# A transformer of three blocks on one core: three weight slots and ten row places while expert rows come, five weight slots elsewhere, and another order in the first up block

## What is computed

```python
def peer_ffn(h, w_q, sub_keys, u_tab, v_tab):
        q = (xc @ w_q).reshape(t, PEER_HEADS, 2, PEER_QDIM // 2)
        sc = jnp.einsum('thpc,hpnc->thpn', q, sub_keys).astype(jnp.float32)
        v_half, i_half = lax.top_k(sc, PEER_TOPK_HALF)
        ...
        top_s, pos = lax.top_k(cand, PEER_TOPK)
        g = jax.nn.softmax(top_s, axis=-1)
        u = u_tab[expert]
        act = jax.nn.gelu(jnp.einsum('thkd,td->thk', u, xc).astype(jnp.float32), approximate=False)
        w = (g * act).astype(xc.dtype)
        return jnp.einsum('thk,thkd->td', w, v_tab[expert])
```

## Time and profile before

| | us |
|---|---|
| median of 3 runs | 2128.93 |
| lowest, highest | 2127.93, 2129.14 |
| profiled execution, device time | 2127.96 |
| span of the profiled execution | 2126.2 |
| PE busy, share of the span | 1665.4 (78%) |
| DVE busy | 1490.8 (70%) |
| ACT busy | 785.7 (37%) |
| POOL busy | 643.3 (30%) |
| DMA moved | 746.87 MB, mean 351 GB/s |
| mean granted clock of PE | 0.902 |

### The profile page before, as it was taken

The page is one execution under the profiler, slowest core; times in us unless marked ns, Lnnn a source line. Parts: engine busy times, 40 slices in busy tenths (PEclk is TensorE's granted clock), DMA queues, the critical chain, the costliest instruction groups (busy, mean ns, idle before and its releaser), DMA issues.

```text
span 2126.2 us, 20672 instructions
## 1 busy us (share of the span) xinstructions
PE 1665.4 (78%) x6490; PEld 1005.3 (47%) x6490; DVE 1490.8 (70%) x3129; ACT 785.7 (37%) x2050; POOL 643.3 (30%) x524
## 2 busy tenths in 40 slices
PE   8797777667777865887778478765767899999998
PEld 4473343622323453333344433554333465668986
DVE  5378876897756688976666897668787465566654
ACT  1213452234424422432452235212555343454432
POOL 0013444335433343643344354425444000000000
PEclk9999989879898987989889799987888999999999
DMA  7358999999999999999999999999999785574452
GB/s 274 148 213 365 421 399 421 419 421 422 418 421 401 416 421 411 413 420 421 416 373 421 412 389 421 421 421 422 400 412 392 308 306 202 194 281 160 178 178 99
DMA packets 105803, 746.87 MB, mean 351 GB/s; under 512 B 12896, under 2 KB 13536, under 8 KB 16608
## 3 DMA queue, kind: packets, MB, share of 16 engines
q0 software_dynamic: 73728, 536.90, 61.4%
q1 hardware_dynamic: 31536, 207.08, 25.1%
q10 hardware_dynamic: 432, 1.57, 0.2%
HBM read 744.46 MB, written 1.05 MB: 351 GB/s over the span
## 4 chain that ended last, share of the span: by engine, by line
PE 39%; DMA 23%; DVE 20%; ACT 10%; issue 6%; DVEq 1%; PEldq 1%; PEld 0%; ACTq 0%; SPq 0%; POOL 0%; POOLq 0%
DMA sb_work<-in_peer_uv,sb_expert 17%; PE ps_acc L1570 11%; PE bank L496 5%; DVE sb_work L1534 5%; PE bank L1363 4%; DVE sb_x L1542 3%; DMA sb_ninth<-in_peer_uv,sb_expert 3%; PE bank L2060 2%; DMA sb_wring<-in_peer_w_q 2%; ACT L1550 2%; PE bank L777 2%; PE bank L566 2%; PE ps_acc L566 2%; PE ps_acc L568 2%; PE ps_acc L567 2%
## 5 line engine op out<-in xcount | busy, mean ns | idle before, releaser
L2694 POOL DMA_INDIRECT sb_work<-in_peer_uv,sb_expert x456 | 567.8, 1245 | 916.8 <-PE ps_acc L1570 401.8
L1570 PE MATMUL ps_acc<-sb_work,sb_diag 128*128 128x512 f32 x1184 | 626.9, 676 | 255.3 <-ACT sb_diag L1559 218.2
L1534 DVE CUSTOM_DVE_ANT_0 sb_work<-sb_work,sb_h 128x1024 f32<-128x1024 f32 x456 | 551.0, 1222 | 147.9 <-DMA sb_work<-in_peer_uv,sb_expert 138.7
L1570 PEld LDWEIGHTS ps_acc<-sb_work,sb_diag 128*128 128x128 f32 x1184 | 242.9, 216 | 586.2 <-issue 577.1
L1550 ACT ACTIVATE sb_dots<-sb_dots 128x1 f32<-128x1 f32 x512 | 102.1, 199 | 501.8 <-DVE sb_dots L1534 471.2
L1542 DVE SCALAR_TENSOR_TENSOR sb_x<-sb_work,sb_weight,sb_x 128x1024 f32<-128x1024 f32 x160 | 205.0, 1281 | 72.3 <-ACT sb_weight L1551 72.3
L560 DVE TENSOR_TENSOR sb_work_r<-sb_wring,sb_work_r 128x2048 fp32r<-128x2048 f32 (+1 forms) x74 | 133.8, 1828 | 101.0 <-ACT sb_work_r L553 100.4
L1551 ACT ACTIVATE sb_weight<-sb_dots,sb_share 128x1 f32<-128x1 f32 x512 | 150.8, 294 | 16.6
L553 ACT CAST sb_work_r<-sb_wring 128x2048 fp32r<-128x2048 f32 (+1 forms) x74 | 111.8, 1536 | 108.8 <-PE ps_acc L568 39.1
L1363 PE MATMUL bank<-sb_hT,sb_wring 128*128 128x128 f32 x1024 | 125.0, 287 | 24.3 <-DMA sb_wring<-in_peer_w_q 21.8
L1363 PEld LDWEIGHTS bank<-sb_hT,sb_wring 128*128 128x128 f32 x1024 | 123.2, 203 | 27.7 <-issue 26.6
(11 more groups left out here) (362 smaller groups left out, 2391.1 us busy)
## 6 DMA issues: line engine op xcount, KB each, us to landing
sb_wring<-in_w_mix SPq DMA_DIRECT2D x36, 1024.0 KB
sb_wring<-in_peer_w_q SPq DMA_DIRECT2D x32, 1024.0 KB
sb_wring<-in_w_gate SPq DMA_DIRECT2D x32, 1024.0 KB
sb_wring<-in_w_up SPq DMA_DIRECT2D x16, 1024.0 KB
sb_wring<-in_w_down SPq DMA_DIRECT2D x16, 1024.0 KB
sb_wring<-in_mla_w_uq SPq DMA_DIRECT2D x12, 768.0 KB
sb_work<-in_hyb_w_in SPq DMA_DIRECT2D x8, 1024.0 KB, 14.7
sb_wring<-in_hyb_w_out SPq DMA_DIRECT2D x8, 1024.0 KB
```

What stands on the lines that cost most here:

```text
L1534: e.tensor_tensor_reduce(u, u, h[:, t, :], 1.0, 0.0, ALU.mult, ALU.add, dots[:, i:i + 1]).then_inc(dot_ready, 1)
L1570: last = e.matmul(ps_acc[:, b * 512:(b + 1) * 512], diag[:, number % DIAGS, :], row(n)[:, D + b * 512:D + (b + 1) * 512], start=k == f["fi ...
L2694: pool.indirect_dma_start(row(n), None, a["peer_uv"], bass.IndirectOffsetOnAxis(ap=expert[:, t, n % P:n % P + 1], axis=0)).then_inc(row_la ...
```

## The change

SLOTS becomes 3. `ninth` becomes `extra` with two pieces of a slot's size, and RING is 10. The two pieces belong to the weight stream before block 20 and from block 104 on, where it has five slots, and to the rows in between, as row places 8 and 9. A new function `place_stream` says for each block into which slot it goes and what it waits for; it takes the slot that was filled longest ago. Rows 8 and 9 wait until the last blocks in the two pieces (18 and 19) are given back, and the first blocks from 104 on in these pieces wait for the last rows there.

```diff
-SLOTS = 4
+SLOTS = 3
+EXTRA = 2
 KEPT = 8
-RING = 9
+RING = KEPT + EXTRA
...
+        def place_stream():
+            last = [None] * (SLOTS + EXTRA)
+            uses = [0] * (SLOTS + EXTRA)
+            for n in range(len(stream)):
+                open_slots = SLOTS if rows_from <= n < rows_until else SLOTS + EXTRA
+                if n == rows_from:
+                    for i in range(EXTRA):
+                        rows_after[KEPT + i] = last[SLOTS + i]
+                if n == rows_until:
+                    for i in range(EXTRA):
+                        last[SLOTS + i] = rows_until - 0.5
+                slot = min(range(open_slots), key=lambda s: -1 if last[s] is None else last[s])
+                if last[slot] == rows_until - 0.5:
+                    n_rows = len(gathers) * P
+                    behind = freed(max(r for r in range(n_rows) if r % RING == KEPT + slot - SLOTS))
+                else:
+                    behind = None if last[slot] is None else given_back[last[slot]]
+                placed[n] = slot, uses[slot], behind
+                last[slot] = n
+                uses[slot] += 1
...
-                if n >= SLOTS:
-                    sp.wait_ge(*given_back[n - SLOTS])
+                if placed[n][2] is not None:
+                    sp.wait_ge(*placed[n][2])
...
                 elif n < KEPT:
                     pool.wait_ge(*given_back["kept", n])
+                else:
+                    pool.wait_ge(*given_back[rows_after[n]])
```

Three smaller edits come with it. In the norm ahead of the first route, PE gets four 128x512 matmuls whose result nobody reads:

```diff
+            def pe(e):
+                for _ in range(4):
+                    e.matmul(ps_scores[:, 0:2, :].rearrange("p a b -> p (a b)"), ident[:, :], busy, start=True, stop=True)
+                p("pe", e)
```

In `project_last` block 7 is split instead of plain:

```diff
-            plain = (9, 0, 3, 7)
+            plain = (9, 0, 3)
```

In the first up block ACT takes the root ahead of its cast and both casts early, and DVE makes the scales ahead of its split:

```diff
             for b, (_, units, sq_v, _) in enumerate(up_plan):
-                split_act(e, next_splits[b][0])
                 if b == 0:
                     e.wait_ge(var_ready.sem, rows_var)
                     e.activation(root, var, ACT.Sqrt).then_inc(root_ready.sem, 1)
-                if b + 1 == len(up_plan):
+                split_act(e, next_splits[b][0])
+                early = b == 0 or b + 1 == len(up_plan)
+                if early:
                     split_act(e, next_splits[b][1])
...
             for b, (_, units, _, hi_v) in enumerate(up_plan):
+                if b == 0:
+                    scale_then(e)
                 split_dve(e, next_splits[b][0])
                 if b == 0:
-                    scale_then(e)
+                    spread_copy(e)
```

More of the change, by code:

```diff
@@ L193, in build @@
         diag = sb("diag", [P, DIAGS, P])
-        ninth = sb("ninth", [P, 2 * D])
-        w_landed = [sem(f"w_landed{i}") for i in range(SLOTS)]
+        extra = sb("extra", [P, EXTRA, SLOT])
+        w_landed = [sem(f"w_landed{i}") for i in range(SLOTS + EXTRA)]
         w_used = Signal(sem("w_used"))
@@ L244, in build @@
         stream = []
+        placed = {}
         given_back = {}
@@ L331, in slot_wait @@
                 return
-            pe.wait_ge(w_landed[n % SLOTS], 16 * (n // SLOTS + 1))
+            slot, use, _ = placed[n]
+            pe.wait_ge(w_landed[slot], 16 * (use + 1))
         def slot_flat(n):
             _, chunks, cols = stream[n]
-            return wring[:, n % SLOTS, 0:chunks * cols]
+            slot = placed[n][0]
+            home = wring[:, slot, :] if slot < SLOTS else extra[:, slot - SLOTS, :]
+            return home[:, 0:chunks * cols]
+        def place_stream():
[18 more added lines that the diff above has]
+                uses[slot] += 1
         def load_table(e, function):
@@ L358, in next_gain, with norm @@
                 load_gain(e, number + 1)
-        def norm(src, dst, width, g, tiles=range(TILES)):
+        def norm(src, dst, width, g, tiles=range(TILES), busy=None):
             act, dve, p, _ = norm_parts(src, dst, width, g, tiles)
-            stage(act=act, dve=dve, points=[p], us=5.0)
+            def pe(e):
+                for _ in range(4):
+                    e.matmul(ps_scores[:, 0:2, :].rearrange("p a b -> p (a b)"), ident[:, :], busy, start=True, stop=True)
+                p("pe", e)
+            stage(pe=None if busy is None else pe, act=act, dve=dve, points=[p], us=5.0)
         def norm_parts(src, dst, width, g, tiles):
@@ L1580, in row @@
         def row(n):
-            return ring[:, n % RING, :] if n % RING < KEPT else ninth[:, :]
+            return ring[:, n % RING, :] if n % RING < KEPT else extra[:, n % RING - KEPT, :]
         def freed(n):
@@ L1642, in feed_forward @@
         def feed_forward(layer, tiles, beside=None, halved=False):
-            norm(X, H, D, (f"ffn{layer}", a["ffn_norm"][layer:layer + 1, :]), tiles)
+            norm(X, H, D, (f"ffn{layer}", a["ffn_norm"][layer:layer + 1, :]), tiles,
+                 hT[:, 0:4, 0:P] if (layer, tiles) == (0, [0]) else None)
             turn_wide(H, hT, DC, tiles)
@@ L2579, in up_act @@
                     e.copy(hidden[0][b][:, j, :], units_2[:, (4 * b + j) % 8, :]).then_inc(turned_hi.sem, 1)
-                if b + 1 < len(up_plan):
+                if not early:
                     split_act(e, next_splits[b][1])
@@ L2603, in scale_then, with spread_copy @@
             last.then_inc(first_row.sem, 1)
+        def spread_copy(e):
             token_unit.wait_full(e)
@@ L2635, in build @@
         share_out()
+        place_stream()
         block = ctx.enter_context(nc.Block())
```

11 lines of the change are left out of this document (6 added, 5 removed).

## The result

The changed kernel takes 2166.65 us (median of 4 runs, 2164.69 to 2173.63) against 2129.03 us (4 runs, 2127.93 to 2130.85). The ratio is 1.0181, with a 95% interval from 1.0164 to 1.0198. That is 37.6 us slower. The prediction said 2156, between 2112 and 2184, and slower at 0.67. The profiled execution took 2165.37 us, with a span of 2163.5.

A forecast was written before the change was run, and what follows sets the result against it. DMA engines near 420 GB/s, with DVE almost full, bound the rows stage; PE the prologue and epilogue. Terms -3, -7.5, +28, +5, +10, -5 gave +27.5 on 2127.96, 2155.5, stated as 2156; range 2112 to 2184.

The forecast's parts named there:

- step E: project_first, nine pairs: three slots lengthen cycles until the row queue empties, then the lag limits itself; +10, 0 to +30.
- A: Prologue's norm: four busy matmuls keep PE's clock up for the first route's first matmuls; -3, between -4 and 0.
- B: Rows stage: tenth place fills gaps in two late windows (-5) and from 290 to 332 (-2.5); -7.5, between -10 and 0.
- The sign named for it: Rows stage: over 410 GB/s in the windows answering to 1500 to 1560 and 1600 to 1640 us.
- C: Three routes beside rows: later pairs wait, ACT's copy and DVE lag 11 each, 3, 2 and 0 hidden; +28, 0 to +40.
- D: Layer 1's two latent projections: w_uq blocks asked for one block's work later; +5 for both, between 0 and +13.
- F: Epilogue: split block 7 (-1.3), scales ahead of the split (-2.3), fifth slot for w_branch (-1.3); -5, between -7 and 0.
- Rival 1: Rows stage: DMA and DVE limit it, so PE's waits are hidden and C, D and E are 0; 2113, chance 0.24.
- Rival 3: Routes and project_first: lag not capped, rows keep half the engines; E +30, C reaches +40; 2190, chance 0.09.
- The case in which double-buffering fails: Three routes: three slots fall short of two pairs, the whole 20 us exposed in each; C 60 less 5, about 2183.

The follow-up runs named there:

- e5_no_busy: e1_four_nine without the four busy matmuls in the norm ahead of the first route; 2120.43 us, ratio 0.9968.
- e11_thirteen: e1_four_nine, but rows 446 to 499 also use the four weight slots, 13 places; 2117.74 us, ratio 0.9954.
- e4_three_in_routes: e1_four_nine with only three slots for the w_q blocks of the three routes beside rows; 2142.01 us, ratio 1.0084.
- e1_four_nine: The changed kernel with four slots and nine row places again while rows come, all else kept; 2117.65 us, ratio 0.9960.
- e9_columns_three: The changed kernel with each w_q block cut as 256 columns of all eight chunks, fetched by two DMAs; 2181.68 us, ratio 1.0251.
- e6_old_up_order: e1_four_nine with the order of before in the first up block; 2121.37 us, ratio 0.9970.
- e7_plain_seven: e1_four_nine with block 7 of project_last plain again; 2116.61 us, ratio 0.9954.

## Why the prediction was right or wrong

The direction and the range were right, and so was the mechanism of the largest term. The sum was 27.5 us and the result 37.4 on the profiled executions; the largest miss, 11.8 us, is step E. Step by step:

- **A, -3.** Right. The clock is 1.00 at the first matmuls and rows start 3.0 us earlier. That this reaches the end is supported by e5_no_busy, but not shown beyond its noise.
- **B, -7.5.** The size was near and the place wrong. With three slots the tenth place brings 7.0 us, with 7 of doubt. But the gain was expected in two late windows, and places there gained nothing (e11_thirteen). The sign named for it failed: over 410 GB/s was expected, and the same stretches, moved by the 44 us by which the rows end later, show 351 and 393. The window from 290 to 332 varies too much to tell.
- **C, +28.** Right, within the 6 us of doubt: 24.4 by e4_three_in_routes. The mechanism is there: waits ahead of all three pairs, pairs at the lower clock, and DVE held up behind ACT's copies. The details differ, and some make up for others. In the second route the fourth pair ends 54 us behind the first in place of the 52.5 said, but by cycles of 19.9, 20.1 and 14.0 us where each was to be 17.5, and the last wait is 4.13, not 7 to 10. DVE's lag arises behind the second pair, not the third, and over both it is 18.2, 10.7 and 11.0 where 11 was said for each. The part that was expected to be hidden behind the first of these routes (3) was larger: 7 us are made up again by the next one.
- **D, +5.** Its waits are there, 5 us more in all, but the rows don't fall back over these stages, so as a term of the time it was about nothing. No run had three slots in the projections alone. What makes the other 9.8 us of three slots with nine places stays open.
- **E, +10.** This is the step that failed; it was 21.8. The prediction said that the lag "limits itself", that after two cycles "blocks come unshared" and that "a cycle is 12.4 or a little more". The cycle never fell. PE's timeline in `project_first` shows the last pairs no shorter than the first. "issue" in the brackets means that the profile names nobody, but these are waits for blocks: SP asks for two when a pair ends, and the median of the landings there is 8.5 us.

```profile
1377.72 10.15 PE L1857 MATMUL bank<-sb_hT,sb_wring 128*128 128x128 f32 x64 [9.83 <-issue]
...
1411.96 10.10 PE L1857 MATMUL bank<-sb_hT,sb_wring 128*128 128x128 f32 x64 [6.71 <-issue]
1429.51 9.87 PE L1857 MATMUL bank<-sb_hT,sb_wring 128*128 128x128 f32 x64 [7.45 <-issue]
...
1479.64 8.75 PE L1857 MATMUL bank<-sb_hT,sb_wring 128*128 128x128 f32 x64 [8.89 <-issue]
1496.98 10.10 PE L1857 MATMUL bank<-sb_hT,sb_wring 128*64 128x128 f32 x64 [8.59 <-issue]
...
1515.61 9.34 PE L1857 MATMUL bank<-sb_hT,sb_wring 128*64 128x128 f32 x64 [4.88 <-issue]
```

From the first pair's start at 1377.72 to the last at 1515.61 the eight cycles take 17.2 us each. Two things were left out. A pair's end frees the weights and, behind ACT's copy, a whole burst of rows. The timelines of ACT, DVE and POOL show it: ACT copies the pair's result, DVE gets the weight that stood behind the copy, and POOL asks for rows 2.3 us apart. This comes right behind the two blocks that SP asks for at 1456.5, after 8 us of idleness:

```profile
1456.52 0.37 ACT L1878 COPY sb_work<-bank 128x256 f32<-128x256 f32 x1 [3.08 <-PE bank L1864]
...
1457.36 1.28 DVE L1576 SCALAR_TENSOR_TENSOR sb_x<-sb_work,sb_weight,sb_x 128x1024 f32<-128x1024 f32 x1 [7.44 <-ACT sb_weight L1585]
...
1458.91 1.68 POOL L2739 DMA_INDIRECT sb_work<-in_peer_uv,sb_expert  x1 [8.19 <-DVE sb_x L1576]
...
1461.25 1.68 POOL L2739 DMA_INDIRECT sb_work<-in_peer_uv,sb_expert  x1 [0.66 <-DVE sb_x L1576]
...
1463.60 1.68 POOL L2739 DMA_INDIRECT sb_work<-in_peer_uv,sb_expert  x1 [0.66 <-DVE sb_x L1576]
```

So a block is shared with rows just when it is wanted, however empty the queue was a moment before. And a wait costs PE its clock: the pair takes 8.8 to 10.2 us in place of 7.4, at a granted clock of 0.70 to 0.84 in the five shown up to 1507. So the 16.7 us that C's arithmetic gave for a cycle were near, and "limits itself" was wrong.

But a cycle of 17.2 is not the whole account. Against the 10.5 us that the prediction took for before, eight such cycles would be 54 us, and 21.8 were lost. The 10.5 were wrong as well: 16 requests in 84 us are eight pairs with seven cycles between, and SP is through with them two pairs before PE is. PE's timeline of before has the first and the ninth pair here:

```profile
1347.27 7.39 PE L1821 MATMUL bank<-sb_hT,sb_wring 128*128 128x128 f32 x64
...
1462.95 10.10 PE L1821 MATMUL bank<-sb_hT,sb_wring 128*64 128x128 f32 x64 [7.04 <-ACT sb_work L1839]
```

That is 14.5 us a cycle. Eight cycles of 2.8 us more are 22, and the wait ahead of the first pair is 9.8 where before there was none. So PE falls back by some 30 us, and 21.8 reach the end. C's cycle for all eight over the 10.5 would have given 50 and missed by more than the 10 did; over the 14.5 it gives 18.

- **F, -5.** Right, a little small: 7.1. The order in the first up block gave 2.9 (said 2.3), block 7 1.3 (said 1.3), the fifth slot 2.9 (said 1.3).

The sum with what was measured is -3 - 7.0 + 24.4 + 9.8 + 21.8 - 7.1 = +38.9, against 37.6 between the medians. The four middle terms make 49.0 by the way they were formed, as differences between e1_four_nine and the changed kernel; what the sum tests is that -3 and -7.1 are the 10 us that e1_four_nine gains.

Rival 1 (the waits are hidden) falls. What spoke for it, that the bytes are the same and the engines full, was true only while something was always queued. Rival 3 named the step and its reason, rows that keep their share while E's pairs wait, and only its sizes (+30, +40) were too large; the prediction set it aside with "must run out". The case in which double-buffering fails priced the routes at the full 20 us; the runs gave 8 each, so more than half was hidden. What hid it, DVE's own work or the queued rows, wasn't separated.

## What to carry to other kernels

Here a buffer that is given back in pairs did well with two pairs of slots. One slot less turned each step into a request, a shared landing and work at a lower clock, and it cost far more than a place elsewhere brought. That the giving back in pairs is the cause fits the timelines but wasn't tested by itself, since e9_columns_three changed the transfers too. Before a lag is called self-limiting, look at what else the same event releases: here the end of a pair let the rival transfers go as well. When the total of buffers is fixed, try both directions; here four and nine beat three and ten by 49 us and five and eight by 13. With the small edits it takes 0.9960 of before, and no kernel of the study is clearly faster. Before a stage's cycle is taken from one engine's requests, look at the engine that does the work: SP asked for a pair every 12 us there, and PE took 14.5 for one.

## What the hardware showed that was not expected

- Two queues with work for the DMA engines share them by packets. In 20 us each got 980 packets, and the one with 1 KB packets got 0.98 MB, the other 7.19. A transfer cut finer costs little by itself (410 against 420 GB/s in all, a fifth more engine time for its own bytes) but starves beside one with large packets.
- In the profiled executions most of the scatter of a kernel's times comes from the rows stage. Kernels that are the same up to there (e1_four_nine, e6_old_up_order, e7_plain_seven) have its end at 1661.07, 1668.10 and 1667.77 us. Eight epilogues that are the same lie within 0.14 us, and two are 1.6 to 1.8 shorter, in e1_four_nine by the clock of one group of products. For an edit of 1 to 3 us, the length of its own stage told more than ten whole runs, once such a step of the clock was seen for what it is.
